# Two layers under an engine loop, or written out one after the other

## The chip, the cores and the metric

One core of one Trainium2 chip runs the whole program. The metric is the device time of one execution in microseconds (us), from the first to the last instruction and what lies around them. The engines are TensorE (PE; its weight loads are PEld), VectorE (DVE), ScalarE (ACT), GpSimd (POOL) and SyncE (SP), which here only issues transfers. Each runs its own stream of instructions; they wait for one another on semaphores.

## What is computed

One sequence of 256 tokens of width 1024 goes through two blocks. The first block (a two-way recurrent mixer, windowed attention and a mixture of experts) isn't touched by the change. The second block is a normalisation and two equal layers with weights of their own:

```python
h = _layer_norm(x, ln_in_g, ln_in_b)
for l in range(DEPTH_2):        # 2 layers
    h = hybrid_layer(h, w_in[l], ..., ln2_b[l])

def hybrid_layer(x, ...):
    (...) = _split(x @ w_in, IN_WIDTHS)
    # four branches: stick-breaking, three-way sparse attention, retention, gated linear attention
    proj = jnp.einsum('bsnc,ncd->bsnd', branches, w_branch)
    mix = jnp.sum(gates * proj, axis=2) @ w_out
    x = _layer_norm(DN_ALPHA * x + mix, ln1_g, ln1_b)
    return _layer_norm(DN_ALPHA * x + peer_ffn(x, peer_wq, peer_keys, peer_u, peer_v), ln2_g, ln2_b)
```

`peer_ffn` scores 8 heads against two tables of 128 keys, takes the best 16 experts per head and token, and sums their rows, weighted by a gelu of a dot product.

## The kernel before

The activations lie in SBUF, channels on partitions, as `xT`. Weights come in tiles of 1 MB (128 partitions of 2048 floats) into `C.ring`, a ring of six. The work is cut into stages. A stage is an object `Stage` (lines 47 to 73) with its own named semaphores and one `nc.Block()`, in which each engine has its instructions. Where a stage ends, `close` clears its semaphores (line 72, on GpSimd) and puts a barrier over all engines (line 73).

`layer` (line 3441) is one layer and has two stages. `mixers` (line 2106) begins with splitting `xT` into a high part on ScalarE (line 2580) and a low part on VectorE (line 2780), eight of each; then the weight halves follow in the same way (lines 2447 and 2607), and TensorE makes three products of each pair (lines 153 to 155). The first product waits for the first low part of the weights. SP loads the tables and masks at the stage's start (lines 2205 to 2211), then the 26 ring tiles that aren't there yet (line 2214), each when VectorE has read the slot's old tile, and three tiles for the merge (line 2220). `merge_peer` (line 2803) multiplies the branches (lines 146 and 153 to 155), finds the experts (lines 3290 to 3337), and fetches their rows: 256 gathers of 1 MB, issued by GpSimd (line 2944), each followed by a dot product on VectorE (line 3404), a gelu and a scaling on ScalarE (lines 3186 and 3192) and products on TensorE (line 3066). At its end SP fetches the first three tiles of the next layer (line 2926).

The two layers aren't written twice. `second_block` (line 3458) opens a loop on the engines:

```python
with C.nc.Fori(0, 2) as l_:
    layer(C, A, l_, xT)
```

Each engine holds the loop's counter in a register of its own, and `l_` is that register. It stands in the addresses of SP's loads, as `A["w_in2"][l_ * TILES2 + n, :, :]` in line 2214, so SP works an address out ahead of each such load. The gathers don't use it: which layer's experts are meant comes as a number from a table (`offset`). The loop's own instructions have line 3459: a jump and a move at its entry, and at its end a step of the counter and a compare-and-branch back to the body's start. The loop is entered behind the first block's last stage (line 1561) and left into the stage that writes the output (line 3491).

The order of work on each engine is written out by hand in both stages; nothing is planned by cost.

Of the kernel before, what the change touches and what calls it, by code (L numbers as in the profile page):

```python
# [14 lines left out]
F32 = mybir.dt.float32  # L15
F32R = mybir.dt.float32r
# [6 lines left out]
P = 128  # L23
D = 1024
KT = D // P
SEQ = 256
# [3 lines left out]
TILE = 2048  # L30
# [100 lines left out]
def load_all(nc, name, pairs):  # L131

    S = Stage(nc, name)
    with nc.Block() as block:
        @block.sync
        def _(sp):
            for dst, src in pairs:
                sp.dma_start(dst, src).then_inc(S["loaded"], 16)
            sp.wait_ge(S["loaded"], 16 * len(pairs))
    S.close()  # L140

# [15 lines left out]

def split_high(S, act, pairs):

    for src, high, low in pairs:  # L160
        act.activation(high, src, ACT.Copy).then_inc(S["acts_high"], 1)

# [1943 lines left out]
def mixers(C, A, l_, v2, V, xT, mg, o, spare):  # L2106
# [5 lines left out]


    nc = C.nc
    S = Stage(nc, "mix")
    GATES = 13
    TS = MIX_AHEAD
    JOBS = 2 * TILES2
# [11 lines left out]
    half = lambda i: slice(CH * i, CH * i + CH)  # L2130

    with ExitStack() as local:
        sb = lambda name, shape, dt=F32: local.enter_context(nc.sbuf_tensor("x_" + name, shape, dt))
        Z = {n: sb(n, [P, 2, SEQ]) for n in ("sq", "sk", "sv", "rq", "rk", "rv", "rg", "gv", "gr", "nq", "nk", "nvx")}
        kcv, gq, gk, gkt = sb("kcv", [P, SEQ]), sb("gq", [P, SEQ]), sb("gk", [P, SEQ]), sb("gkt", [P, SEQ])
        lr = sb("lr", [32, SEQ])
# [2 lines left out]
        w2 = sb("weights", [P, 4, 2, TILE // 2], F32R)  # L2139
# [663 lines left out]
def merge_peer(C, A, l_, V, x1, mg, o, zh, spare):  # L2803
# [2 lines left out]


    nc = C.nc
    S = Stage(nc, "peer")
    NB = 4  # L2810
    PAIR = KT // 2
    bank = C.bank
# [23 lines left out]
    y = flat(3).rearrange("p (t c) -> p t c", t=TT)  # L2836
    z = [mg[:, i * KT:(i + 1) * KT, :].rearrange("p a t -> p (a t)") for i in range(4)]
    with ExitStack() as local:
        sb = lambda name, shape, dt=F32: local.enter_context(nc.sbuf_tensor(name, shape, dt))
        with ExitStack() as under:  # L2840
            mh = under.enter_context(nc.sbuf_tensor("merged_halves", [P, 2, KT, SEQ], F32R))
            w2 = under.enter_context(nc.sbuf_tensor("merge_weights", [P, 4, 2, TILE // 2], F32R))
        over = sb("uv_rows", [P, 6, TILE])
        keys = sb("peer_keys", [P, 2 * PH, KEYS])
        wq = sb("query_weights", [P, 4, TILE])
# [595 lines left out]
def layer(C, A, l_, xT):  # L3441
    nc = C.nc
    with ExitStack() as outer:
        so = lambda name, shape: outer.enter_context(nc.sbuf_tensor(name, shape, F32))
        v2 = so("vec2", [P, VEC2_COLS])
        spare = so("spare", [P, KT, SEQ])
        V = {name: v2[:, at:at + n] for name, (at, n) in VEC2_AT.items()}
        with ExitStack() as mid:
            sm = lambda name, shape: mid.enter_context(nc.sbuf_tensor(name, shape, F32))
            with ExitStack() as under:  # L3450
                zh = under.enter_context(nc.sbuf_tensor("w_out_halves", [P, 5, 2, TILE // 2], F32R))
            mg = sm("z_mg", [P, 4 * KT, SEQ])
            o = sm("z_o", [P, 8, SEQ])
            mixers(C, A, l_, v2, V, xT, mg, o, spare)
            merge_peer(C, A, l_, V, xT, mg, o, zh, spare)


def second_block(C, A, xT):
    with C.nc.Fori(0, 2) as l_:
        layer(C, A, l_, xT)  # L3460


# [7 lines left out]
def build(nc, A, out):  # L3470
    with ExitStack() as ctx:
        C = Core(nc, ctx)
        square = C.keep("square", [P, len(SQUARE), P])
        C.sq = {k: square[:, i, :] for i, k in enumerate(SQUARE)}
        epst = C.keep("eps", [P, len(EPS)])
        C.eps = [epst[:, i:i + 1] for i in range(len(EPS))]
        C.masks = C.keep("masks", [P, 5, CH])
        vec = C.keep("vec", [P, VEC_COLS])
        C.v = {}
        for name, (at, n) in VEC_AT.items():  # L3480
            C.v[name] = vec[:, at:at + n]
        xT = C.keep("xT", [P, KT, SEQ])
        consts = [(square[:, :, :], A["square"]), (epst[:, :], A["eps"]), (C.masks[:, :, :], A["masks"]),
                  (vec[:, :], A["vec"]), (xT[:, :, :], A["xT"])]
        first_block(C, A, xT, consts)
        second_block(C, A, xT)
        S = Stage(nc, "end")
        with nc.Block() as block:
            @block.sync
            def _(sp):  # L3490
                sp.dma_start(out, xT[:, :, :]).then_inc(S["out"], 16)
                sp.wait_ge(S["out"], 16)
        S.close()
# [159 lines left out]
```

## Time and profile before

| what | us |
|---|---|
| median of 3 runs | 3024.58 |
| all 3 runs | 3015.12, 3024.58, 3026.96 |
| the profiled execution, its own time | 3016.59 |
| its span, first to last instruction | 3014.5 |
| TensorE, VectorE, ScalarE, GpSimd busy | 2629.2, 1989.2, 1178.7, 659.1 |

The span covers the first block up to about 1054, layer 0 up to 2030.5, and layer 1 up to 3010. Busy time is an average over stages with different limits; what a change in one place is worth is read from what waits for what there. A wait booked to "issue" is time in which an engine stood still and the profile shows nothing that it waited for. The names of tensors are printed without their numbers: `in_w_in` in a row of the second block is `w_in2`, and `vec` is `vec2`.

### The profile page before, as it was taken

Reading aid. Unit: us, or ns where it says so; the run is one execution under the profiler, and the core shown is the slowest. Engines: PE = TensorE matmul, PEld = TensorE weight load, DVE = VectorE, ACT = ScalarE, POOL = GpSimd, SP = SyncE. Lnnn points to the kernel's source line nnn. Section 1 sums busy time; section 2 is a strip of 40 time slices with the busy share of each in tenths; the row PEclk is TensorE's granted clock in tenths of the full one; section 3 lists DMA queues with packets and bytes.
Section 4 is the critical chain, followed back from the end, with each engine's and each line's share of the span. In section 5 each row is a group of like instructions: output and inputs, shape, how many; then the busy total and the mean of one; then the engine's idle time right before and its main releaser. Section 6 shows DMA issues by size and latency. Waiting matters only on the chain. (4 is left out here: it accounts for less than half of the span.)

```text
span 3014.5 us, 44102 instructions
## 1 busy us (share of the span) xinstructions
PE 2629.2 (87%) x17284; PEld 1865.9 (62%) x17284; DVE 1989.2 (66%) x4149; ACT 1178.7 (39%) x2267; POOL 659.1 (22%) x570
## 2 busy tenths in 40 slices
PE   7999888879999789998998778778999898877876
PEld 3896778778888689985544333337998554433332
DVE  3556656458999756657767777645665776767764
ACT  3334544437888554532222222225453222222222
POOL 0001000000003200004444444420000444444442
PEclk8999999989999999999999999989999999999999
DMA  6551000228999453448999999984344899999998
GB/s 274 208 224 43 3 3 3 106 113 316 370 374 368 189 178 125 154 196 358 420 400 421 421 422 421 422 332 161 134 154 196 358 421 402 421 421 422 421 421 334
DMA packets 120915, 838.85 MB, mean 278 GB/s; under 512 B 15386, under 2 KB 18236, under 8 KB 19588
## 3 DMA queue, kind: packets, MB, share of 16 engines
q0 software_dynamic: 77600, 564.43, 45.5%
q1 hardware_dynamic: 43108, 271.59, 24.1%
q8 instruction: 139, 2.28, 0.3%
q14 instruction: 68, 0.56, 0.1%
HBM read 834.65 MB, written 1.05 MB: 277 GB/s over the span
## 5 line engine op out<-in xcount | busy, mean ns | idle before, releaser
L3066 PE MATMUL bank<-uv_rows,z_o 128*128 128x512 f32 x840 | 416.8, 641 | 86.0 <-ACT z_o L3192 85.8
L3066 PEld LDWEIGHTS bank<-uv_rows,z_o 128*128 128x128 f32 x840 | 166.9, 204 | 311.8 <-issue 197.1
L3404 DVE CUSTOM_DVE_ANT_0 uv_rows<-uv_rows,ring 128x1024 f32<-128x1024 f32 x210 | 255.4, 1224 | 144.6 <-DMA uv_rows<-in_peer_uv,peer_index 144.5
L3066 PE MATMUL bank<-query_weights,z_o 128*128 128x512 f32 x584 | 289.7, 646 | 67.8 <-ACT z_o L3192 67.7
L2944 POOL DMA_INDIRECT uv_rows<-in_peer_uv,peer_index x210 | 236.3, 1125 | 387.3 <-PE bank L3066 241.1
L1798 DVE TENSOR_TENSOR moe_halves<-ring,moe_halves 128x1024 fp32r<-128x1024 f32 x240 | 285.7, 1222 | 29.6 <-ACT moe_halves L1722 27.0
L3186 ACT ACTIVATE peer_gelu<-peer_act 128x4 f32<-128x4 f32 (+2 forms) x134 | 27.5, 205 | 693.3 <-DVE peer_act L3404 693.3
L3066 PE MATMUL bank<-z_mg,z_o 128*128 128x512 f32 x504 | 234.9, 610 | 45.0 <-ACT z_o L3192 45.0
L1722 ACT ACTIVATE moe_halves<-ring 128x1024 fp32r<-128x1024 f32 x240 | 249.0, 1059 | 42.3 <-PE bank L155 42.0
L3192 ACT ACTIVATE z_o<-square,peer_wts 128x128 f32<-128x128 f32 x512 | 164.4, 391 | 254.2 <-DVE peer_wts L3416 237.7
L153 PE MATMUL bank<-x_halves,x_weights 128*128 128x256 f32 x800 | 235.6, 295 | 30.4 <-DVE x_weights L2607 27.9
L3066 PEld LDWEIGHTS bank<-query_weights,z_o 128*128 128x128 f32 x584 | 117.2, 206 | 226.8 <-issue 139.0
L3404 DVE CUSTOM_DVE_ANT_0 query_weights<-query_weights,ring 128x1024 f32<-128x1024 f32 x146 | 177.4, 1224 | 103.1 <-DMA query_weights<-in_peer_uv,peer_index 103.1
L2607 DVE TENSOR_TENSOR x_weights<-ring,x_weights 128x1024 fp32r<-128x1024 f32 x116 | 140.7, 1224 | 158.2 <-ACT x_weights L2447 157.7
L154 PE MATMUL bank<-x_halves,x_weights 128*128 128x256 f32 x800 | 228.5, 286 | 0.0
L155 PE MATMUL bank<-x_halves,x_weights 128*128 128x256 f32 x800 | 228.3, 285 | 0.0
L2944 POOL DMA_INDIRECT query_weights<-in_peer_uv,peer_index x146 | 170.1, 1165 | 215.9 <-PE bank L3066 175.1
L3404 DVE CUSTOM_DVE_ANT_0 z_mg<-z_mg,ring 128x1024 f32<-128x1024 f32 x126 | 153.3, 1223 | 85.6 <-DMA z_mg<-in_peer_uv,peer_index 85.4
L3066 PEld LDWEIGHTS bank<-z_mg,z_o 128*128 128x128 f32 x504 | 95.5, 194 | 168.1 <-issue 108.7
L2447 ACT ACTIVATE x_weights<-ring 128x1024 fp32r<-128x1024 f32 x116 | 121.9, 1056 | 180.0 <-PE bank L155 180.0
L2944 POOL DMA_INDIRECT z_mg<-in_peer_uv,peer_index x126 | 152.1, 1207 | 143.1 <-PE bank L3066 133.4
L153 PEld LDWEIGHTS bank<-x_halves,x_weights 128*128 128x128 f32 x800 | 155.6, 195 | 37.7 <-issue 34.1
(634 smaller groups left out, 5739.3 us busy)
## 6 DMA issues: line engine op xcount, KB each, us to landing
ring<-in_moe SPq DMA_DIRECT2D x96, 1024.0 KB, 7.0
ring<-in_w_in SPq DMA_DIRECT2D x83, 1024.0 KB, 5.0
ring<-in_mod_rows SPq DMA_DIRECT2D x16, 1024.0 KB, 4.8
ring<-in_w_out SPq DMA_DIRECT2D x12, 1024.0 KB, 8.7
ring<-in_mod_w SPq DMA_DIRECT2D x8, 1024.0 KB, 11.5
ring<-in_w_branch SPq DMA_DIRECT2D x8, 1024.0 KB, 8.7
query_weights<-in_peer_wq SPq DMA_DIRECT2D x8, 1024.0 KB, 10.4
ring<-in_peer_wq SPq DMA_DIRECT2D x6, 1024.0 KB, 5.6
```

Of the source, the lines that this page charges most:

```text
L153: pe.matmul(out, a[0], b[0], start=first, stop=False)
L154: pe.matmul(out, a[0], b[1], start=False, stop=False)
L155: return pe.matmul(out, a[1], b[0], start=False, stop=last)
L1722: act.activation(w2[:, p % 4, 0, :], C.ring[:, n % RING, COLUMNS[c]], ACT.Copy)\
L1798: dve.tensor_tensor(w2[:, p % 4, 1, :], C.ring[:, n % RING, COLUMNS[c]], w2[:, p % 4, 0, :].bitcast(F32), ALU.subtract).then_inc(S["low"], 1)
L2447: act.activation(w2[:, p % 4, 0, :], C.ring[:, n % TS, COLUMNS[c]], ACT.Copy).then_inc(S["high"], 1)
L2607: dve.tensor_tensor(w2[:, p % 4, 1, :], C.ring[:, n % TS, COLUMNS[c]], w2[:, p % 4, 0, :].bitcast(F32), ALU.subtract).then_inc(S["low"], 1)
L2944: pool.indirect_dma_start(out=row(j), out_offset=None, in_=A["peer_uv"], in_offset=bass.IndirectOffsetOnAxis(ap=index[:, g, k:k + 1], axis ...
L3066: ins = pe.matmul(bank[2 * t + c][:, :], diag[:, q % 2, i, :], row(j)[:, D + c * 512:D + (c + 1) * 512], start=(j % (PH * TOPK) == 0), sto ...
L3186: act.activation(gel[:, q % 2, 0:size], acts[:, g % 2, c:c + size], ACT.Gelu).then_inc(S["gelu"], 1)
L3192: ins = act.activation(diag[:, q % 2, n, :], C.sq["ident"], ACT.Copy, scale=wts[:, q % 2, n:n + 1])
L3404: dve.tensor_tensor_reduce(u, u, xtok[:, t, :], 1.0, 0.0, ALU.mult, ALU.add, acts[:, g % 2, j % TOPK:j % TOPK + 1]).then_inc(S["dots"], 1)
```

## The change

The loop is taken out. A loop of the program that builds the kernel takes its place: `layer` is called twice, with `l_` 0 and 1 as plain numbers. The body stands in each engine's stream twice, one behind the other. Since names must differ, each layer's memory and semaphores get `l_` in their names; sizes and the order in which memory is taken and given back stay.

```diff
@@ mixers
-    S = Stage(nc, "mix")
+    S = Stage(nc, f"mix{l_}")
...
-        sb = lambda name, shape, dt=F32: local.enter_context(nc.sbuf_tensor("x_" + name, shape, dt))
+        sb = lambda name, shape, dt=F32: local.enter_context(nc.sbuf_tensor(f"x_{name}_{l_}", shape, dt))
@@ merge_peer
-    S = Stage(nc, "peer")
+    S = Stage(nc, f"peer{l_}")
...
-        sb = lambda name, shape, dt=F32: local.enter_context(nc.sbuf_tensor(name, shape, dt))
+        sb = lambda name, shape, dt=F32: local.enter_context(nc.sbuf_tensor(f"{name}_{l_}", shape, dt))
         with ExitStack() as under:
-            mh = under.enter_context(nc.sbuf_tensor("merged_halves", [P, 2, KT, SEQ], F32R))
-            w2 = under.enter_context(nc.sbuf_tensor("merge_weights", [P, 4, 2, TILE // 2], F32R))
+            mh = under.enter_context(nc.sbuf_tensor(f"merged_halves_{l_}", [P, 2, KT, SEQ], F32R))
+            w2 = under.enter_context(nc.sbuf_tensor(f"merge_weights_{l_}", [P, 4, 2, TILE // 2], F32R))
@@ layer
-        so = lambda name, shape: outer.enter_context(nc.sbuf_tensor(name, shape, F32))
+        so = lambda name, shape: outer.enter_context(nc.sbuf_tensor(f"{name}_{l_}", shape, F32))
...
@@ second_block
-    with C.nc.Fori(0, 2) as l_:
+    for l_ in range(2):
         layer(C, A, l_, xT)
```

ScalarE at the end of layer 0, before. The last row is the loop's branch; the rows above it are the last normalisation of the layer.

```order
L3216 ACTIVATE ring<-ring,peer_shift,peer_spread 128x512
L3146 ACTIVATE xT<-bank,vec 128x128 x4
L2899 UNCONDITIONAL_BRANCH
L3459 REGISTER_ALU
L3459 COMPARE_AND_BRANCH
```

The same place on ScalarE in the changed kernel:

```order
L3216 ACTIVATE ring<-ring,peer_shift,peer_spread 128x512
L3146 ACTIVATE xT<-bank,vec_0 128x128 x4
L2899 UNCONDITIONAL_BRANCH
L2439 UNCONDITIONAL_BRANCH
L2580 ACTIVATE x_halves<-xT 128x256 x8
L2447 ACTIVATE x_weights<-ring 128x1024 x5
```

The counter's step and the branch back are gone, and layer 1's first halves follow directly. It is the same on the other four engines.

SP where layer 0 begins, before (an ISA row is the address worked out in registers):

```order
L1561 UNCONDITIONAL_BRANCH
L3459 UNCONDITIONAL_BRANCH
L2203 UNCONDITIONAL_BRANCH
L2205 DMA x_causal<-in_causal 128x512
L2208 ISA
L2208 DMA ring<-in_cmp_w 128x2048
L2208 ISA
L2208 DMA x_cmp_pos<-in_cmp_pos 128x32
L2208 DMA x_cmp_bias<-in_cmp_bias 128x120
```

And in the changed kernel:

```order
L1561 UNCONDITIONAL_BRANCH
L2203 UNCONDITIONAL_BRANCH
L2205 DMA x_causal<-in_causal 128x512
L2208 DMA ring<-in_cmp_w 128x2048
L2208 DMA x_cmp_pos<-in_cmp_pos 128x32
L2208 DMA x_cmp_bias<-in_cmp_bias 128x120
```

The loop's entry and the address work ahead of each load that depends on the layer are gone, here and at lines 2211, 2214, 2220, 2903, 2906, 2910, 2913 and 2926.

## Rows read from the trace of the kernel before

**Rows 1.** The page: span, engines, and the chain that ended last.
```profile
span 3014.5 us, 44102 instructions
...
DMA 11%; PE 9%; DVE 3%; ACT 1%; issue 1%; POOL 0%; another core or an unknown queue 0%; DVEq 0%
```

**Rows 2.** Stages by time: busy time per engine, granted clock, DMA share, GB/s.
```profile
1054.00:2030.50 976.50, 845.23 (x3794) 536.70 (x3794) 641.43 (x1508) 310.10 (x698) 298.52 (x260) 0.95 0.81 329
2030.50:3010.00 979.50, 840.77 (x3794) 534.19 (x3794) 641.66 (x1508) 310.03 (x698) 303.08 (x260) 0.95 0.81 328
...
1295.20:1364.80 69.60, 69.49 (x376) 61.03 (x376) 46.42 (x105) 18.87 (x32) 2.95 (x4) 0.96 0.57 219
...
1364.80:2017.40 652.60, 542.74 (x1513) 261.07 (x1514) 452.26 (x1171) 160.82 (x446) 293.74 (x253) 0.94 0.99 411
```

**Rows 3.** Sequencers where layer 0 begins, line 73 (barrier): length ns, first and last start.
```profile
L73 ACTq EVENT_SEMAPHORE  x1: 17/17/17, 1054.7 to 1054.7; - x1
```

**Rows 4.** Timeline there: start, length, engine, line, operation, [idle before].
```profile
1055.11 2.56 ACT L2580 ACTIVATE x_halves<-xT 128x256 fp32r<-128x256 f32 x8 [2.42 <-PEq L73]
...
1055.56 2.77 DVE L2780 TENSOR_TENSOR x_halves<-xT,x_halves 128x256 fp32r<-128x256 f32 x8 [3.44 <-ACT x_halves L2580]
1058.65 3.50 DVE L2607 TENSOR_TENSOR x_weights<-ring,x_weights 128x1024 fp32r<-128x1024 f32 x3 [0.32 <-ACT x_weights L2447]
...
1060.02 0.55 PE L153 MATMUL bank<-x_halves,x_weights 128*128 128x256 f32 x1 [13.49 <-DVE x_weights L2607]
```

**Rows 5.** Sequencers where layer 0 ends, lines 73 and 3459.
```profile
L73 ACTq EVENT_SEMAPHORE  x1: 17/17/17, 2030.6 to 2030.6; - x1
...
L3459 ACTq COMPARE_BRANCH  x1: 55/55/55, 2030.7 to 2030.7; - x1
...
L3459 PEldq COMPARE_BRANCH  x1: 3572/3572/3572, 2030.9 to 2030.9; - x1
L3459 SPq MOVE  x1: 34/34/34, 2031.1 to 2031.1; - x1
```

**Rows 6.** Timeline where layer 1 begins.
```profile
2034.16 2.56 ACT L2580 ACTIVATE x_halves<-xT 128x256 fp32r<-128x256 f32 x8 [5.70 <-issue]
...
2034.61 1.10 DVE L2780 TENSOR_TENSOR x_halves<-xT,x_halves 128x256 fp32r<-128x256 f32 x3 [5.43 <-ACT x_halves L2580]
2039.10 1.77 DVE L2780 TENSOR_TENSOR x_halves<-xT,x_halves 128x256 fp32r<-128x256 f32 x5 [3.39 <-issue]
2040.78 4.62 DVE L2607 TENSOR_TENSOR x_weights<-ring,x_weights 128x1024 fp32r<-128x1024 f32 x4
...
2042.14 0.55 PE L153 MATMUL bank<-x_halves,x_weights 128*128 128x256 f32 x1 [14.37 <-DVE x_weights L2607]
```

**Rows 7.** Code on DMA queue q8 (packets, MB): layer 0, then layer 1.
```profile
q8 instruction: 30, 0.49, 0.2%
...
q8 instruction: 32, 0.52, 0.2%
```

**Rows 8.** The stage start behind the mixers of layer 0, and its barrier.
```profile
L73 ACTq EVENT_SEMAPHORE  x1: 17/17/17, 1295.0 to 1295.0; - x1
...
1295.07 0.31 ACT L3150 ACTIVATE alpha_ident<-square 128x128 f32<-128x128 f32 x1 [1.96 <-PEq L73]
```

**Rows 9.** Register work ahead of the ring loads on SP, line 2214.
```profile
L2214 SPq FUSED_REGOPS  x52: 46/46/71, 1061.0 to 2247.6; - x52
L2214 SPq MOVE ring<-in_w_in x52: 29/29/29, 1061.2 to 2247.6; - x52
```
**Rows 10.** Granted clock before and after TensorE resumes in layer 1, then layer 0.
```profile
2046.00:2048.00 2.00, 2.00 (x11) 2.00 (x11) 0.00 (x0) 0.35 (x1) 0.00 (x0) 0.50 1.05 426
...
1064.00:1066.00 2.00, 2.00 (x14) 2.00 (x14) 0.00 (x0) 0.52 (x1) 0.00 (x0) 0.68 1.00 397
```

**Rows 11.** Waits with no releaser ("issue"), whole run: us, times, longest.
```profile
DVE peer_chosen L3306 <- issue: 0.3, 2, 0.2
...
ACT z_o L3192 <- issue: 6.4, 2, 3.2
```

More of the change, by code:

```diff
@@ L3448, in layer @@
         with ExitStack() as mid:
-            sm = lambda name, shape: mid.enter_context(nc.sbuf_tensor(name, shape, F32))
+            sm = lambda name, shape: mid.enter_context(nc.sbuf_tensor(f"{name}_{l_}", shape, F32))
             with ExitStack() as under:
-                zh = under.enter_context(nc.sbuf_tensor("w_out_halves", [P, 5, 2, TILE // 2], F32R))
+                zh = under.enter_context(nc.sbuf_tensor(f"w_out_halves_{l_}", [P, 5, 2, TILE // 2], F32R))
             mg = sm("z_mg", [P, 4 * KT, SEQ])
```

## The prediction

> **What bounds the kernel.** I read the page first, then the stretches, then the two places where a layer begins. The page gives a span of 3014.5 us for 44102 instructions and a chain of waits that ends last with DMA ahead of TensorE [rows 1]; no engine is the bound everywhere. The table of stretches gives one row to each pass of the loop: 976.5 us for layer 0 and 979.5 us for layer 1, with the same number of instructions on every engine [rows 2]. Inside a layer TensorE sets the pace of the merge (69.49 busy of 69.60 us), and the gathers of the experts' rows, 652.6 us at a DMA share of 0.99, are paced by transfers [rows 2]. The change touches no instruction of these stretches but SP's register work. What it touches is the seam: the branch back at the loop's end, the start of the body behind it, the jump into the loop and the way out.
>
> So the two starts of the same code are laid side by side. Layer 0 is entered from straight code, so it shows how the stage starts without a branch back. Its barrier releases ScalarE at 1054.7 [rows 3]; ScalarE starts the first halves at 1055.11, VectorE runs all eight subtractions in one piece and begins the weights' low parts at 1058.65, and TensorE's first product stands at 1060.02 [rows 4]. Layer 1 is entered through the branch. The barrier releases ScalarE at 2030.6 and its compare-and-branch stands at 2030.7 [rows 5]; then nothing runs, and the wait is booked to "issue", that is to nothing the profile shows, until 2034.16. VectorE does three subtractions, is silent for 3.39 us ("issue" again), does the other five, and begins the low parts at 2040.78; TensorE starts at 2042.14 [rows 6]. TensorE's own branch record lasts 3572 ns [rows 5], about as long as ScalarE's silence. SP alone is quick: its first register move is at 2031.1 [rows 5].
>
> I read this as code being fetched anew after the branch: once for the branch's target on ScalarE and TensorE, and on VectorE again a few instructions on. Queue q8 moves 0.49 MB of code in layer 0 and 0.52 MB in layer 1 [rows 7], so the second pass is fetched, not kept. Straight code gets there ahead of time, since the engine waits at its barrier while code flows in.
>
> **The change, term by term.** All against the profiled execution.
>
> 1. ScalarE's start of layer 1. Before: 2034.16, which is 3.56 us behind the barrier's release at 2030.6. After: layer 0 needs 1055.11 - 1054.7 = 0.41 us [rows 3, 4], the start of a stage without a loop's entry 1295.07 - 1295.0 = 0.07 us [rows 8]. The gain lies between 3.15 and 3.49 us. I take 3.3, the middle: the new seam has no loop entry, as the second row, but many rows begin here at once, as in the first.
>
> 2. VectorE's second silence. From ScalarE's first half to VectorE's first low part it is 2040.78 - 2034.16 = 6.62 us in layer 1 and 1058.65 - 1055.11 = 3.54 us in layer 0 [rows 4, 6]. The difference, 3.08 us, is the silence of 3.39 less 0.31 that layer 0 waits for ScalarE. Lower bound 0 (the silence stays), upper bound 3.08; I take 3.1, since layer 0 is the same code without a branch ahead of it. The product waits for exactly this low part in both layers (its releaser is VectorE, line 2607), so terms 1 and 2 add up on the path.
>
> 3. The loop's entry ahead of layer 0: one jump and one register move on each engine. 0.41 against 0.07 us [rows 3, 8] bounds it by 0.34 from above and by nothing from below; I take 0.15.
>
> 4. The way out: the counter's step and the compare that isn't taken, ahead of the output's transfer. On the way round ScalarE needs 55 ns for the compare [rows 5] and the counter's step stands just before it; I take 0.1 us.
>
> 5. SP's register work. Each ring load of line 2214 loses two instructions, 46 + 29 = 75 ns, 52 times in both layers, in all 3.9 us on SP [rows 9]; 24 further loads in each layer's code have the same, 48 x 75 ns = 3.6 us. I cost it at nothing. The cover is TensorE, which paces the mixers' tiles (ScalarE waits for its products, not for loads) and is busy 69.49 of 69.60 us in the merge [rows 2]. If the cover were gone, the ceiling is 7.5 us. The gathers are issued by GpSimd and use no loop register.
>
> 6. New names and semaphores: memory is handed out in the same order and given back between the layers, and each stage clears its semaphores as before, in the same number of clears. Nothing, in either direction.
>
> Does the gain survive? Downstream of TensorE's start everything in layer 1 hangs on the same work, and the gathers cannot start before the scores. The clock could give some back. TensorE resumes at half speed: the granted clock is still 0.50 (1.2 GHz) until 2048, 6 us behind its start, in layer 1; in layer 0 it rises within 1064 to 1066, 4 to 6 us behind its start [rows 4, 6, 10]. Both stretches follow an idle TensorE, and so will the new one. A microsecond more or less at half speed is half a microsecond of work: 0.5 us either way.
>
> Sum: 3.3 + 3.1 + 0.15 + 0.1 = 6.65 us. The profiled execution took 3016.59 us (span 3014.5), so the same execution would take 3009.9. The four executions shown lie at 3015.12, 3016.59, 3024.58 and 3026.96; their spread of 11.8 us is larger than the gain. The profiled one is among the low ones; against the median of 3024.58 the sum would be 3017.9. With three and one executions the middle is poorly known, so I take the mean of all four, 3020.8, less 6.65: **3014.2 us**.
>
> **A rule weighed.** The rows show 55 ns for ScalarE's branch and 3.4 us of silence behind it [rows 5, 6]. The Trainium skill (Advanced Engine Details and Errata, Control Flow Timing) gives about 108 ns for a compare-and-branch and about 51 ns for a plain one. By these alone the change would be worth about 0.3 us and not 6.65; that case stands among the rivals. The rule prices the instruction; what stands behind it the trace prices at over ten times that.
>
> **The rivals.**
>
> - *Only the first silence goes.* VectorE's second one is tied to where a piece of code ends, or to the loads that SP issues at that moment (tables, masks and a ring tile), and appears again. For it: layer 1's body lies elsewhere in the program now. Against it: the same loads run in layer 0 with no silence. Then 3.3 + 0.25 = 3.55 us: 3017.3. Chance 0.15.
> - *The branch is innocent.* Both silences have another cause that stays, and only entry and exit go, 0.3 us: 3020.5. Against it: TensorE's branch record is itself 3572 ns long [rows 5]. Chance 0.06.
> - *SP's register work counts.* Term 5 lies on the path after all, in part or whole, as far as 6.65 + 7.5 = 14.15 us: 3006.7. Against it: the cover named there. Chance 0.05.
> - *Slower: the longer straight program runs dry.* In layer 1 the pieces of code end at other instructions than in the loop. Where a fetch comes late under full DMA, in the gathers above all, VectorE or TensorE stands for a silence like those seen, 3.4 us each, ahead of work that every later gather waits for. For it: ScalarE has one of 3.2 us in each layer, in straight code, within the gathers ahead of line 3192 [rows 11], where DMA is at 0.99. Against it: VectorE's largest other total is 0.3 us over the whole run [rows 11], and layer 0 is straight code of the same length. Two such silences on the path cancel the gain, seven make it slower by over 0.5%. With four: -6.65 + 13.6 = +7.0 us, 3027.8. The Trainium skill (Runtime: NRT & Kernel Launch, Instruction fetch mechanics) says that crossing from one piece of code to the next is mostly hidden; by that this rival is worth nothing, and no run here shows it for a program of this length. Chance 0.08.
>
> That the loop stays in some form is excluded: on every engine the branch is gone and the body stands twice.
>
> **How the numbers follow.** The forecast keeps 0.66. Range: the low end is the forecast less 10 us, which takes in most of the way to the register rival and the spread of executions; the high end is the first two rivals plus about 5 us of that spread. 3004 to 3025. About 0.5% of the time, 15 us, is what a measurement of this kernel can tell from no change. The forecast and its first two rivals lie within it. Faster by more needs the register rival at its ceiling or luck with the executions: 0.04. Slower by more needs seven silences: 0.03. Within: 0.93.
>
> **What would show it.** Right: ScalarE's first half of layer 1 within 0.5 us of the barrier; eight subtractions in one piece; TensorE's product 5 to 5.5 us behind the barrier instead of 11.5; no branch record of 3.6 us; layer 1's stretch near 973 us, layer 0's near 976.5; gathers still near 652 us at 0.99. Wrong: a new wait on "issue" over 1 us on VectorE or TensorE, or a gather stretch longer than 656 us. A layer 1 that keeps 979 us would say that the seam's gain is eaten later.

## The result and the profile after

| | before | changed |
|---|---|---|
| median of 20 runs, us | 3022.80 | 3016.89 |
| lowest and highest, us | 3015.12 and 3029.59 | 3009.02 and 3021.76 |
| profiled execution's span, us | 3014.5 | 3017.0 |
| layer 0, layer 1 (barrier to barrier), us | 975.9, 979.0 | 975.5, 975.6 |

The ratio of changed to before is 0.998 with a 95% interval of 0.9973 to 0.9987, that is 3.9 to 8.2 us less. The forecast was 3014.2, in a range of 3004 to 3025.

From the page of the changed kernel, and its two layers in the table of stretches (for [rows 1, 2]):

```profile
span 3017.0 us, 43875 instructions
...
DMA 10%; PE 10%; DVE 3%; ACT 1%; issue 1%; POOL 0%; another core or an unknown queue 0%; DVEq 0%; POOLq 0%
...
1061.00:2036.50 975.50, 847.05 (x3794) 537.61 (x3794) 641.40 (x1508) 310.21 (x698) 297.60 (x260) 0.94 0.81 329
2036.50:3012.50 976.00, 844.00 (x3794) 537.43 (x3794) 641.32 (x1508) 310.30 (x698) 296.86 (x260) 0.94 0.81 329
```

The profiled execution is longer than that of before although the change is faster. Its first block, the same code in both, ended at 1061.1 in place of 1054.7: 6.4 us more, as much as the whole gain. Two single traces don't show the gain in their spans; the pieces do. The rows of the stretches are cut up to 0.7 us beside the barriers; between the barriers themselves layer 0 lost 0.4 us and layer 1 3.4 us. Layer 1's start, which this takes in, became 6.5 us shorter, so behind its first product the layer took 3.1 us longer than before. That is taken up below (e9).

The seam, for [rows 5, 6]: ScalarE's barrier, then the timeline of ScalarE, VectorE and TensorE.

```profile
L73 ACTq EVENT_SEMAPHORE  x1: 17/17/17, 2036.6 to 2036.6; - x1
...
2036.69 2.56 ACT L2580 ACTIVATE x_halves<-xT 128x256 fp32r<-128x256 f32 x8 [2.23 <-PEq L73]
...
2037.14 2.77 DVE L2780 TENSOR_TENSOR x_halves<-xT,x_halves 128x256 fp32r<-128x256 f32 x8 [1.96 <-ACT x_halves L2580]
2040.23 4.63 DVE L2607 TENSOR_TENSOR x_weights<-ring,x_weights 128x1024 fp32r<-128x1024 f32 x4 [0.32 <-ACT x_weights L2447]
...
2041.60 0.55 PE L153 MATMUL bank<-x_halves,x_weights 128*128 128x256 f32 x1 [7.83 <-DVE x_weights L2607]
```

ScalarE starts 0.09 us behind the barrier (3.56 before). VectorE does its eight subtractions in one piece. The first product stands 5.0 us behind the barrier, where it stood 11.5.

The traces also hold the transfers of code themselves, on the queues q8 and q14 (packets, MB; a packet doesn't say for which engine it is). In the kernel before, in ScalarE's silence (2030.60 to 2034.16) and in VectorE's (2035.71 to 2039.10):

```profile
q8 instruction: 1, 0.02, 2.0%
q14 instruction: 2, 0.02, 1.7%
...
q8 instruction: 1, 0.02, 2.5%
q14 instruction: 2, 0.02, 1.1%
```

Between the two silences (2034.16 to 2035.71) there is none. In the changed kernel there is none on either queue from the barrier at 2036.6 to the first product at 2041.6. So each silence has code arriving in it, and the seam without silences has none.

The start of layer 0, for [rows 4], on ScalarE and TensorE, behind a barrier at 1061.1:

```profile
1061.44 2.56 ACT L2580 ACTIVATE x_halves<-xT 128x256 fp32r<-128x256 f32 x8 [2.35 <-PEq L73]
...
1066.35 0.55 PE L153 MATMUL bank<-x_halves,x_weights 128*128 128x256 f32 x1 [13.41 <-DVE x_weights L2607]
```

That is 0.34 us for ScalarE (0.41 before) and 5.25 for TensorE (5.3). Two waits on "issue" on ScalarE in this trace, for [rows 11]:

```profile
ACT peer_gelu L3186 <- issue: 9.2, 1, 9.2
...
ACT z_o L3192 <- issue: 7.3, 3, 3.2
```

The silence of 9.2 us in the gathers of layer 1 isn't in the two later traces of the same kernel, and ScalarE's silences ahead of line 3192 stand in some traces and not in others, whatever the kernel, so neither is put down to the change. TensorE has one of 2.4 us in the gathers of layer 0 (ahead of line 3066 at 1545.29), which the trace of before hasn't; it isn't in the two later traces either.

### The profile page after: what moved, and what is told of

Its sections match the earlier page's. It is cut to its first block and busy times, and to the rows that moved or that the text cites. A ratio compares the mean times of both kernels' runs of the same rounds, so it can differ in the third digit from the quotient of the medians.

```text
span 3017.0 us, 43875 instructions
## 1 busy us (share of the span) xinstructions
PE 2640.2 (88%) x17284; PEld 1874.3 (62%) x17284; DVE 1988.8 (66%) x4149; ACT 1179.2 (39%) x2267; POOL 652.0 (22%) x570
## 5 line engine op out<-in xcount | busy, mean ns | idle before, releaser
L3066 PE MATMUL bank<-z_mg,z_o 128*128 128x512 f32 x504 | 246.0, 634 | 51.0 <-ACT z_o L3192 50.9
```

The lines of the kernel that those rows point to most:

```text
L3066: ins = pe.matmul(bank[2 * t + c][:, :], diag[:, q % 2, i, :], row(j)[:, D + c * 512:D + (c + 1) * 512], start=(j % (PH * TOPK) == 0), sto ...
```

## The experiments

Each edit is against the kernel before or the changed kernel, as named. "Seam" is the time from the barrier that ends layer 0 to the first product of layer 1.

| run | what it is | ScalarE after barrier | seam | ratio to before |
|---|---|---|---|---|
| before, first trace | loop | 3.56 | 11.5 | |
| e9 | loop, again | 2.8 | 10.7 | 1.0000 (0.9989 to 1.0010) |
| e1, e5, e11 | loop with the hint | 0.7 | 5.6 | 0.9996 (0.9986 to 1.0006), 0.9996 (0.9983 to 1.0009) |
| e2 | loop, VectorE's body placed | 3.6 | 8.5 | one execution |
| e3 | loop, hint, all bodies placed | 0.7 | 5.6 | 0.9998 (0.9989 to 1.0008) |
| changed, e6, e10 | unrolled | 0.1 | 5.0 | 0.998, 0.9989 (0.9980 to 0.9998), 0.9975 (0.9964 to 0.9987) |
| e4 | unrolled, forward jump | 4.2 | 9.2 | one execution |
| e7 | unrolled, registers on SP | 0.1 | 5.0 | 0.9993 (0.9984 to 1.0002) |
| e8 | unrolled, short loop (from its last barrier) | 0.2 | 5.1 | one execution |
| e12 | unrolled, other start order | 0.1 | 2.9 | 0.9950 (0.9935 to 0.9965) |

### Loop with a hint (e1)

```diff
-    with C.nc.Fori(0, 2) as l_:
+    with C.nc.Fori(0, 2, hint_back_edge=True) as l_:
```

The hint is one instruction per engine at the body's start that names the branch at its end.

> The loop stays; a hint at the body's start names the branch at its end, so that the code at the branch's target can be fetched before the branch is taken. Theory 1 (the first silence is the target's code being fetched after the branch): ScalarE's first half of layer 1 comes 0.1 to 0.5 us behind the barrier instead of 3.56, and TensorE's branch record shrinks from 3572 ns to under 200. VectorE's second silence of 3.39 us may stay, since a hint names one place only; then the first product stands 8.0 to 8.5 us behind the barrier (before 11.5, changed 5.0), and if it goes too, 5.0. Rival (the silences come from something else at the seam, such as the loads that start there): both stay, 11.5 us.

TensorE's branch record, ScalarE's barrier, and the timeline:

```profile
L3459 PEldq COMPARE_BRANCH  x2: 93/251/409, 2027.1 to 2999.1; - x2
...
L73 ACTq EVENT_SEMAPHORE  x1: 17/17/17, 2026.9 to 2026.9; - x1
...
2027.59 2.56 ACT L2580 ACTIVATE x_halves<-xT 128x256 fp32r<-128x256 f32 x8 [2.86 <-PEq L73]
...
2028.04 2.77 DVE L2780 TENSOR_TENSOR x_halves<-xT,x_halves 128x256 fp32r<-128x256 f32 x8 [2.59 <-ACT x_halves L2580]
...
2032.50 0.55 PE L153 MATMUL bank<-x_halves,x_weights 128*128 128x256 f32 x1 [8.46 <-DVE x_weights L2607]
```

Both silences went; whether the second would was left open. ScalarE's 0.7 us and TensorE's branch record of 409 ns (3572 before) are a little above what was expected, and so is the seam, 5.6 us against the unrolled kernel's 5.0. Code still arrives behind the barrier (between 2026.9 and 2032.5 one packet on q8 and two on q14), but no engine stands still for it. The loop, its counter and SP's register work are all still there, so the rival (the silences come from the loads that start at the seam) is out: SP issues the same loads at the same place. The single time of 3008.91 says little: the lowest of before beside it was 3008.45.

### Only VectorE's body placed (e2)

```diff
-    with C.nc.Fori(0, 2) as l_:
+    with C.nc.Fori(0, 2, head_slot={mybir.EngineType.DVE: 0}) as l_:
```

VectorE's body begins at the first place of a block of code as it is fetched. Queue q8 moves 0.49 MB in 30 packets, 16 KB each [rows 7]; the Trainium skill (Runtime: NRT & Kernel Launch, Instruction fetch mechanics) has the same 16 KB and counts 256 instructions in it.

> The loop stays; only VectorE's loop body is placed so that it begins at the start of a block of code and not near the end of one. Theory 1 (the second silence is the fetch of the next block, which begins right behind the branch's target): the first silence stays on every engine (ScalarE 3.5 us behind the barrier), VectorE runs all eight subtractions in one piece, and the first product stands 8.4 us behind the barrier (11.5 less 3.1). Rival (the second silence comes from loads or another engine): VectorE still stands 3.4 us after three subtractions, 11.5 us in all.

```profile
L73 ACTq EVENT_SEMAPHORE  x1: 17/17/17, 2030.7 to 2030.7; - x1
...
2034.31 2.56 ACT L2580 ACTIVATE x_halves<-xT 128x256 fp32r<-128x256 f32 x8 [5.71 <-issue]
...
2034.76 2.77 DVE L2780 TENSOR_TENSOR x_halves<-xT,x_halves 128x256 fp32r<-128x256 f32 x8 [5.44 <-ACT x_halves L2580]
...
2039.22 0.55 PE L153 MATMUL bank<-x_halves,x_weights 128*128 128x256 f32 x1 [11.31 <-DVE x_weights L2607]
```

As theory 1 has it, to 0.1 us: ScalarE's silence stays whole, VectorE's second one is gone, and the seam is 8.5 us. The q8 packet of VectorE's silence is gone too: between 2034.31 and 2038.5 q8 moves nothing, q14 two packets. I read the second silence as the fetch of the next block of code, needed right behind the target because the target lay near its block's end; that it goes when the body's place changes fits this, but no trace shows where in its block the target lay. The two silences are two fetches, and the second can be taken out by itself.

### Hint and all bodies placed (e3)

```diff
-    with C.nc.Fori(0, 2) as l_:
+    heads = {e: 0 for e in mybir.ALL_ENGINES}
+    with C.nc.Fori(0, 2, hint_back_edge=True, head_slot=heads) as l_:
```

> The loop stays, with the hint and with the body placed at the start of a block of code on every engine. Theory 1: both silences go, the first product stands 5.0 to 5.5 us behind the barrier as in the unrolled kernel, and the ratio to the kernel before is 0.998, 6 us less. Rival (what helps is the unrolled code itself, such as the loads without registers or the missing counter): the ratio stays at 1.000.

ScalarE at the start of layer 0 (barrier, jump, first half) with VectorE's first instruction behind its own jump, then the seam (barrier, first product):

```profile
L73 ACTq EVENT_SEMAPHORE  x1: 17/17/17, 1060.4 to 1060.4; - x1
...
L3460 ACTq COMPARE_BRANCH  x1: 38/38/38, 1060.8 to 1060.8; - x1
...
L3460 DVEq BRANCH_PREFETCH_HINT  x1: 56/56/56, 1061.1 to 1061.1; - x1
...
1064.57 2.56 ACT L2580 ACTIVATE x_halves<-xT 128x256 fp32r<-128x256 f32 x8 [6.15 <-issue]
...
L73 ACTq EVENT_SEMAPHORE  x1: 17/17/17, 2037.5 to 2037.5; - x1
...
2043.11 0.55 PE L153 MATMUL bank<-x_halves,x_weights 128*128 128x256 f32 x1 [8.44 <-DVE x_weights L2607]
```

The seam is 5.6 us, but the time isn't 6 us less; on the face of it the rival's outcome. The trace shows where it went: placing the bodies makes every engine jump over padding when it enters the loop, and on ScalarE and SP this jump is a fetch as well (the first instruction behind it comes 3.7 and 3.1 us later). TensorE, VectorE and GpSimd are behind theirs within 0.6 us, and in e2 VectorE's jump at the entry cost nothing either. ScalarE starts layer 0 4.2 us behind its barrier in place of 0.4, and the first product there stands at 9.1 us (1069.48, behind 1060.4) in place of 5.3. The seam's 5.9 us less 3.8 leaves a gain of 2.1 us, inside the interval, which goes from 3.3 us less to 2.4 us more. ScalarE's silence was moved from one end of the loop to the other.

### A forward jump in the unrolled kernel (e4)

```diff
     for l_ in range(2):
+        if l_:
+            flag = C.nc.alloc_registers("never")
+            C.nc.regs_mov(flag, 0)
+            with C.nc.If_eq(flag, 1):
+                for _ in range(300):
+                    C.nc.all_engine_barrier()
         layer(C, A, l_, xT)
```

> The unrolled kernel with one test between the layers whose body (300 barriers, never run) is jumped over, so that every engine takes one forward jump at the seam and there is no loop. No part of the computation changes. Theory 1 (any jump to code that isn't there yet costs a fetch, forward or back): ScalarE's first half of layer 1 stands 3 to 4 us behind the last barrier instead of 0.1, and the first product 8 to 12 us behind it, according to where the target lies in its block. Rival (only a loop's branch back costs, or the register work around it): 0.2 to 0.6 us and 5.0 to 5.5 us.

ScalarE's barrier, the jump on ScalarE and TensorE, and the timeline:

```profile
L73 ACTq EVENT_SEMAPHORE  x1: 17/17/17, 2029.5 to 2029.5; - x1
...
L2203 ACTq COMPARE_BRANCH  x1: 50/50/50, 2029.6 to 2029.6; - x1
...
L2203 PEldq COMPARE_BRANCH  x1: 3630/3630/3630, 2029.7 to 2029.7; - x1
...
2033.75 2.56 ACT L2580 ACTIVATE x_halves<-xT 128x256 fp32r<-128x256 f32 x8 [6.42 <-issue]
...
2038.66 0.55 PE L153 MATMUL bank<-x_halves,x_weights 128*128 128x256 f32 x1 [12.02 <-DVE x_weights L2607]
```

There is no loop here, and the silence is back: 4.2 us on ScalarE (3 to 4 expected), 3630 ns on TensorE's jump, with one packet of code on q8 and four on q14 between 2029.5 and 2033.75. SP stood as well this time (its first load came 4.1 us behind the barrier; before it was 0.6). So it isn't the branch back, the counter or the register work; a jump to code that isn't at hand costs a fetch. The Trainium skill (Runtime: NRT & Kernel Launch, Instruction fetch mechanics) states this for taken branches whose target lies outside the window of code an engine holds. These traces agree, with 2.8 to 4.2 us for it on ScalarE; how large that window is no run here shows.

### The hint timed (e5, e11), the unrolled kernel again (e6, e10), before against itself (e9)

The kernels are those of e1, the change, and before, unedited.

> The looped kernel with the hint alone, timed. In its single look the first product of layer 1 stood 5.6 us behind the barrier (before 11.5). Theory 1 (the time saved is the two fetches and nothing else): 11.54 - 5.6 = 5.9 us less than the kernel before, ratio 0.998, within 1 us of the unrolled kernel of this same call. Rival (the unrolled code gains elsewhere too): ratio near 1.000, or clearly above that of the unrolled kernel.

> The changed kernel once more, on the same chip as the run with the hint. Theory 1: ratio 0.998, 6.5 us less at the seam and 0.2 us at entry and exit. If the wait of 9.2 us on ScalarE in the gathers and its three of about 3 us, seen in the first trace of the changed kernel, belong to the unrolled code, they are here again; if they belong to that execution, they are not.

> The kernel before against itself: what the comparison tells from no change, and a second trace of it. Ratio 1.000 with about 0.001 either way. Theory 1: seam 11.5 us from barrier to first product again. Layer 1 from its first product to the first load for the layer behind it took 954.2 us in the first trace of before, and 955.1 to 957.3 in the traces with a short seam on that session's and the later chip. Rival (a short seam is paid back by 2 to 3 us later in the layer): again 954 here, with 956 to 957 in the next two runs. If it is chance (the clock), it is 956 to 957 here as well.

> The changed kernel a third time, beside before on the same chip. Theory 1: 6.7 us less, ratio 0.9978; by the two intervals so far it lies between 0.998 and 0.999. Rival (part is paid back): 3 to 5 us less, ratio 0.9985 to 0.999.

> The loop with the hint, timed once more. Theory 1: 5.9 us less by the seam, ratio 0.998, within 1 us of the unrolled kernel; the first timing gave 0.9996 (0.9986 to 1.0006), which just leaves that out. Rival (a loop with the hint loses elsewhere what it gains at the seam): ratio 0.9996 again, at least 2 us above the unrolled kernel of this call.

The unrolled kernel was 3.3 us (0.6 to 6.0) and 7.5 us (3.9 to 10.8) faster, with 5.9 us in the first comparison. The mean of the three is 5.6 us; e6's interval ends short of the 6.7 us of seam, entry and exit. The rival (part is paid back) is neither shown nor out: a payback of 1 to 2 us would fit as well. How much of the seam arrives at the next barrier, between the mixers and the merge of layer 1, the traces tell: it stands 245.4 and 245.1 us behind the seam's barrier in the two traces of before, 240.2, 239.7 and 239.7 in the unrolled kernel's, 240.5, 240.6 and 241.0 with the hint. So between 4.9 and 5.7 us of the seam's gain are still there in the unrolled kernel, and between 4.1 and 4.9 with the hint.

The hint is the miss. Its seam is 5.6 us in all three traces, so 5.9 us should be gained, and twice the ratio was 0.9996, 1.2 us, both intervals ending short of 5.9 (at 4.2 and 5.1). Beside the unrolled kernel it was 2.4 and 6.9 us slower, where the seams differ by 0.6. Its traces show no place for it: the layers from first product to the load for the next layer took 956.5 and 957.3 us in e5 (unrolled, e6: 957.0 and 955.1), and 952.4 and 953.0 in e11 (unrolled, e10: 951.6 and 952.8).

The times on record show where 3 us of it are: outside the span. An execution's time is longer than its span, from first to last instruction, by 2.0 to 2.1 us in the median for every other kernel here (single executions 1.7 to 3.4), and by 5.1 and 5.2 us for the looped kernel with the hint in e5 and e11 (single executions 4.0 to 5.9), with 5.2 in e1. By the median spans the hint's kernel is 4.1 and 2.2 us below before (3014.7 against 3018.8, and 3008.2 against 3010.4), and 1.2 us below and 3.5 above the unrolled kernel; such medians are good to about 3 us, so what is left inside the span can be chance. What the 3 us outside it are stays open, since no trace reaches there; in e3, with the hint and the bodies placed, they are absent (1.9 us).

Before against itself gave a ratio of 1.0000 with 0.001 either way. Its trace has the seam once more, a little shorter (10.7 us). Layer 1 from its first product to the load behind it took 950.1 us, against 952.8 and 953.0 in the two traces beside it (e10, e11): by the figures written down beforehand this is the rival's pattern (a short seam is paid back), not that of chance. But e2 and e4, with seams of 8.5 and 9.2 us, took 953.8 and 953.2 there, and e1 and e3, with 5.6 us, 953.1 and 954.5; so a long seam isn't paid back as such. And the trace has something else, in the merge's first 6 us in layer 0 and layer 1:

```profile
2036.32 2.56 ACT L2580 ACTIVATE x_halves<-xT 128x256 fp32r<-128x256 f32 x8 [4.91 <-issue]
...
2036.81 1.10 DVE L2780 TENSOR_TENSOR x_halves<-xT,x_halves 128x256 fp32r<-128x256 f32 x3 [4.69 <-ACT x_halves L2580]
2041.15 1.77 DVE L2780 TENSOR_TENSOR x_halves<-xT,x_halves 128x256 fp32r<-128x256 f32 x5 [3.25 <-issue]
...
1301.90:1307.90 6.00, 6.00 (x15) 4.81 (x16) 0.69 (x1) 0.22 (x1) 0.05 (x1) 0.52 0.79 298
2278.80:2284.80 6.00, 6.00 (x28) 5.30 (x29) 2.00 (x3) 0.22 (x1) 0.05 (x1) 1.00 0.82 299
```

ScalarE's silence and VectorE's stop after three subtractions are as in [rows 6]. The last two rows are the same code in the two layers. In layer 0 the granted clock is 0.52 over the 6 us (1.2 GHz nearly throughout) and 15 products are issued, in layer 1 it stayed at 1.00 (2.4 GHz) and there are 28. TensorE had stood idle about 3.5 us ahead of both. From the merge's first load to its last three query tiles the stretch took 23.90 us in layer 0 and 21.03 in layer 1; over all traces it lies between 21.0 and 24.0, in any kernel. In both traces of before it was layer 1 that had luck here (22.72 and 21.03 against 23.84 and 23.90). From first product to the layer's end the two layers differ by 3.1 us in the first trace, of which this is 1.1, and by 2.5 us in e9, where this, with 2.9, accounts for all of it. In the changed kernel's three traces layer 1 had 22.56, 21.03 and 23.53. With two traces of before I can't tell whether a longer seam moves the point at which the clock falls, or whether it was chance.

### Unrolled, with SP's registers (e7)

```diff
-    for l_ in range(2):
-        layer(C, A, l_, xT)
+    for NAME[0] in range(2):
+        counter = C.nc.alloc_registers(f"layer_{NAME[0]}")
+        C.nc.regs_mov(counter, NAME[0])
+        layer(C, A, C.nc.snap(counter, min_val=0, max_val=1), xT)
```

The names of memory and semaphores take `NAME[0]`, the plain number; the addresses of SP's loads take the register.

> The unrolled kernel, but SP gets the layer's number from a register again, so that each load that depends on the layer has its two register instructions (about 100 loads, 75 ns each, 7.5 us on SP in all). No jump, no loop. Theory 1 with term 5 at nothing: seam 5.0 us, same time as the unrolled kernel of this call within 1.5 us, ratio 0.998. Rival (SP's register work counts): up to 7.5 us more than the unrolled kernel, ratio up to 1.0003.

Seam 5.0 us. The median was 3019.33, against 3017.96 for the unrolled kernel beside it (e6) and 3021.04 for before: 1.4 us more than the unrolled kernel, and by the two intervals at most about 5. The ceiling of 7.5 us is out. The next barrier of layer 1 stands 240.2 us behind the seam's, as in the changed kernel's first trace; term 5 was rightly put at nothing or near it.

### A short loop between the layers (e8)

```diff
     for l_ in range(2):
+        if l_:
+            with C.nc.Fori(0, 9):
+                C.nc.all_engine_barrier()
         layer(C, A, l_, xT)
```

> The unrolled kernel with a short loop of nine passes over one barrier put between the layers, so that every engine takes eight branches back to code it has just run. Theory 1 (a branch costs a fetch only where its target's code has been overwritten or was never there): a pass costs the barrier (about 1.2 us by the one at 2029.5 to 2030.6) and 0.1 to 0.3 us for counter and branch, 9 to 15 us in all, and the first product stands 5 to 6 us behind the last barrier. Rival (every taken branch back costs about 3.4 us): eight times more, 38 to 45 us in all.

The loop's compare-and-branch on ScalarE and TensorE (nine each), and the start behind it:

```profile
L3461 ACTq COMPARE_BRANCH  x9: 40/45/50, 2038.5 to 2044.2; - x9
...
L3461 PEldq COMPARE_BRANCH  x9: 76/208/232, 2038.6 to 2044.3; - x9
...
2044.25 2.56 ACT L2580 ACTIVATE x_halves<-xT 128x256 fp32r<-128x256 f32 x8 [8.56 <-PEq L3462]
...
2049.16 0.55 PE L153 MATMUL bank<-x_halves,x_weights 128*128 128x256 f32 x1 [14.16 <-DVE x_weights L2607]
```

Nine branches between 2038.5 and 2044.2 are 0.71 us a pass, the barrier in it: even less than expected. Behind the last branch the first product stands 5.0 us. No code is fetched from the loop's start to the first product (no packet on q8 or q14 between 2037.9 and 2049.16). Eight branches back to code at hand cost nothing that the trace shows beyond the instruction itself, 45 ns on ScalarE and 208 on TensorE. The rival (every taken branch costs 3.4 us) is out: the whole pass is a fifth of that.

### The first weights ahead of the activations (e12)

```diff
@@ mixers, TensorE
-                pe.wait_ge(S["acts_low"], KT)
...
                     for k in range(KT):
+                        if j == 0:
+                            pe.wait_ge(S["acts_low"], k + 1)
@@ mixers, ScalarE
+                high(0)
                 for k in range(KT):
                     act.activation(xh[:, 0, k, :], xT[:, k, :], ACT.Copy).then_inc(S["acts_high"], 1)
-                for p in range(4):
+                for p in range(1, 4):
                     high(p)
@@ mixers, VectorE: the same, with low
```

> The unrolled kernel with another order at each layer's start: the first weight half goes ahead of the eight halves of the activations on ScalarE and VectorE, and TensorE takes the activations' pieces one by one as they come. The first product then waits for one weight half (1.04 and 1.22 us) and one piece (0.40 and 0.42 us) and not for eight pieces: it stands 2.7 to 3.1 us behind the barrier in place of 5.0 (layer 1) and 5.3 (layer 0), 4.5 us less in all. If TensorE sets the pace from there, the ratio is 0.9965, 11 us less than before. Rival (the next weight half comes as late as ever, and TensorE waits for it behind the first job): the first product is early, the time is that of the unrolled kernel.

ScalarE's barrier, VectorE (here lines 2609 and 2783) and TensorE:

```profile
L73 ACTq EVENT_SEMAPHORE  x1: 17/17/17, 2023.9 to 2023.9; - x1
...
2025.06 1.22 DVE L2609 TENSOR_TENSOR x_weights<-ring,x_weights 128x1024 fp32r<-128x1024 f32 x1 [2.60 <-ACT x_weights L2448]
2026.20 2.77 DVE L2783 TENSOR_TENSOR x_halves<-xT,x_halves 128x256 fp32r<-128x256 f32 x8
...
2026.76 0.55 PE L153 MATMUL bank<-x_halves,x_weights 128*128 128x256 f32 x1 [5.71 <-DVE x_halves L2783]
```

The first product stands 2.9 us behind the barrier (5.0), and in layer 0 3.2 us (5.25). TensorE waits for no second weight half behind it. The ratio is 0.9950 (0.9935 to 0.9965): 15 us less than before by the ratio and 12.4 by the medians (3000.1 and 3012.5), and 6.6 us below the unrolled kernel beside it (e10), where the two starts explain 2.1 + 2.1 = 4.2; the rest is within the intervals. This kernel beats both.

## Why the prediction was right

- **ScalarE's start (term 1).** 3.3 us were put down, with 3.15 and 3.49 as bounds. It measured 3.56 - 0.09 = 3.47, at the upper bound: the new seam behaves like the stage start without a loop's entry. The bounds came from one trace of before; against the second (e9) it is 2.8 - 0.1 = 2.7, below the lower one.
- **VectorE's second silence (term 2).** 3.1 us; measured 6.62 - 3.54 = 3.08. That it is code and not the loads, e2 shows: it went with nothing but VectorE's code moved, and the packet of code that had arrived in it went too. That terms 1 and 2 add up on the path, e2's seam shows (8.5 us, one gone).
- **Entry and exit (terms 3 and 4).** 0.15 and 0.1 us. Entry: 0.41 to 0.34 us, so 0.07. Exit: the output's load is issued 0.27 us behind the barrier before (3009.87 behind 3009.6), 0.1 after (3012.30 behind 3012.2), so 0.17. Together as put down.
- **SP's registers (term 5).** Put at nothing; e7 has 1.4 us, which its intervals can't tell from nothing or from 5.
- **The sum.** 6.65 us; by the pieces of the first traces 3.47 + 3.08 + 0.07 + 0.17 = 6.8, against e9's seam 5.9, and by the executions' times 5.9 (3.9 to 8.2). The base was the weaker number: the mean of four executions was 3020.8, while the median of twenty was 3022.8. Most of the 2.7 us between forecast and measurement is this.
- **The clock.** It was put at 0.5 us either way, too little. Behind the changed seam the granted clock was 0.82 over the first 8 us, behind the entry of layer 0 in the same execution 0.67:

```profile
2041.60:2049.60 8.00, 8.00 (x56) 8.00 (x57) 4.49 (x4) 3.44 (x5) 0.00 (x0) 0.82 1.01 382
...
1066.40:1074.40 8.00, 8.00 (x47) 8.00 (x48) 4.43 (x4) 2.72 (x4) 0.00 (x0) 0.67 0.98 392
```

In layer 1 it rose 3.0 us behind the first product, in layer 0 5.4 us. Over the traces it is 3 to 6, so about 1.6 us of work hang on it at each start, and up to 3 us at the merge (21.0 to 24.0). Such differences and the first block's 6 us are of the size of the spread of executions.

- **The signs written down.** ScalarE's start, the eight subtractions, the first product at 5.0 us and the missing branch record came as forecast. Layer 1's stretch near 973 us didn't: it was 976.0. e2 and e4, by single traces, speak against a payback of a short seam; in both traces of before layer 1 was the quicker one behind its first product (e9). A new wait of 2.4 us on TensorE, a sign of being wrong, stood in the first trace alone.

- **The rivals.** That only the first silence goes and that the branch is innocent are out (the trace of the change; e4). That SP's registers count is out at its size (e7). That the longer straight program runs dry isn't seen: VectorE and TensorE have no new silence that comes back from trace to trace. The figure of about 108 ns for a compare-and-branch (the Trainium skill, Advanced Engine Details and Errata, Control Flow Timing) is above what the rows show on ScalarE (40 to 55 ns) and below TensorE's 208 ns with the target at hand (e8), so it holds in kind there; where the target isn't at hand, ScalarE's traces show 2.8 to 4.2 us on top.

## What to carry to other kernels

A loop on the engines whose body's start is no longer at hand when it branches back, as here after 976 us of other code, costs a fetch of its code, and a second where the body begins (as I read e2) near the end of a block of code; a loop short enough to stay at hand costs neither (e8). Read it as "issue" behind the branch, and as a branch record of microseconds on TensorE. With two passes there is one such branch, worth 6 us, so unroll if the program may grow, and look at the start of the body first: what stands between the barrier and the first product is paid in every pass, loop or no loop, and reordering it brought as much again. Placing or padding code can move the fetch to the next jump, as it did on ScalarE and SP in e3 and didn't on the other engines. And compare whole execution times as well as traces: a change can cost outside the span, as the hint did with 3 us.

## What the runs showed that I had not expected

- One hint for the branch took away both silences, though it names one place only (e1).
- The same hint was worth 5.9 us at the seam and 1.2 us by the execution times, twice. Of the difference 3 us lie outside the span, where no trace reaches.
- ScalarE's silence behind the same branch was 3.56 us in one trace of before and 2.8 in the other, and 4.2 behind the jumps of e3 and e4.
- The gathers, from the first to the load for the next layer, took 655 to 658 us in one set of traces (before, changed, e5 to e8) and 651 to 653 in another (e1 to e4, e9 to e12), for all kernels of the set alike. ScalarE's silence of about 3.2 us ahead of line 3192 stands in every trace of the first set and in none of the second. Compare only what ran together.
